# Low halves of twelve weight quarters computed on GpSimd inside the long-convolution layer, and one transposed block sent to other PSUM banks

## The reference, cut to what matters

```python
def hyena_mixer(h, w_in, short_w, short_b, f_w1, ..., f_skip, w_out):
    v, x1, x2 = jnp.split(depthwise_conv3(h @ w_in, short_w, short_b), 3, axis=-1)
    h_freq = hyena_filters(seq, f_w1, f_b1, f_w2, f_b2, f_w3, f_freq)   # divided by the sum of |filter|
    def long_conv(u, n):
        uf = u.astype(jnp.float32)
        y = jnp.fft.irfft(jnp.fft.rfft(uf, n=2 * seq, axis=1) * h_freq[:, n], n=2 * seq, axis=1)[:, :seq]
        return (y + uf * f_skip[n].astype(jnp.float32)).astype(u.dtype)
    z = x1 * long_conv(v, 0)
    z = x2 * long_conv(z, 1)
    return z @ w_out
```

## Time and profile before

| | us |
|---|---|
| median of 3 runs | 2025.57 |
| lowest, highest | 2024.82, 2026.21 |
| the profiled execution: time | 2027.8 |
| the profiled execution: span from first to last instruction | 2026.0 |
| PE busy in the span | 1970.8 |
| DVE busy | 1275.4 |
| ACT busy | 907.7 |
| GpSimd busy | 159.6 |
| load of a weight quarter (`w_raw`), median from issue to landing | 3.5 |

### The profile page before, as it was taken

One profiled execution on the slowest core, in us unless ns is written; L12 is line 12 of the kernel. 1 busy time (PEld: TensorE's weight loads), 2 busy tenths in 40 slices (PEclk: granted clock), 3 DMA queues, 4 the chain that ended last, 5 costly groups with the idle time before them and its releaser, 6 DMA issues.

```text
span 2026.0 us, 30699 instructions
## 1 busy us (share of the span) xinstructions
PE 1970.8 (97%) x12630; PEld 1608.2 (79%) x12630; DVE 1275.4 (63%) x1623; ACT 907.7 (45%) x1284; POOL 159.6 (8%) x198
## 2 busy tenths in 40 slices
PE   7999999999899999999999999999999999999999
PEld 6689788877678878888878678877767888898887
DVE  7874855567765565755767655577886555475554
ACT  4452344435444434444545444434434444444442
POOL 2242100000010010000002011002100000000000
PEclk9999999999999999999999999999998999999999
DMA  8411365646156654565565347553332566454554
GB/s 297 123 53 56 103 215 195 219 155 209 53 172 207 223 177 169 175 188 186 166 198 187 111 129 225 198 187 125 104 125 88 182 197 218 158 196 156 186 168 154
DMA packets 93044, 335.97 MB, mean 166 GB/s; under 512 B 11230, under 2 KB 11364, under 8 KB 92623
## 3 DMA queue, kind: packets, MB, share of 16 engines
q1 hardware_dynamic: 85824, 311.62, 46.3%
q0 software_dynamic: 7120, 22.95, 4.2%
HBM read 332.43 MB, written 1.05 MB: 165 GB/s over the span
## 4 chain that ended last, share of the span: by engine, by line
PE 87%; DVE 8%; ACT 2%; POOL 1%; issue 1%; DMA 0%; SPq 0%; DVEq 0%; ACTq 0%; POOLq 0%
PE acc L420 43%; PE acc L506 20%; PE acc L477 8%; DVE w_lo L1658 2%; PE acc L978 2%; PE aux L899 1%; PE aux L526 1%; PE aux L683 1%; POOL rstd L2494 1%; DVE w_spare_lo L1658 1%; PE aux L966 1%; PE aux L934 1%; POOL rstd L2497 1%; PE acc L670 1%; DVE operand_lo L1685 1%
## 5 line engine op out<-in xcount | busy, mean ns | idle before, releaser
L1658 DVE TENSOR_TENSOR w_lo<-w_raw,w_hi 128x1024 fp32r<-128x1024 f32 x552 | 670.3, 1225 | 531.4 <-ACT w_hi L1238 527.9
L1238 ACT ACTIVATE w_hi<-w_raw 128x1024 fp32r<-128x1024 f32 x552 | 580.2, 1059 | 719.2 <-PE acc L420 445.8
L420 PE MATMUL acc<-w_hi,operand_hi 128*128 128x512 f32 x1232 | 489.4, 397 | 14.6 <-DVE operand_lo L1832 12.4
L420 PE MATMUL acc<-w_hi,operand_lo 128*128 128x512 f32 x1232 | 482.3, 391 | 0.0
L420 PE MATMUL acc<-w_lo,operand_hi 128*128 128x512 f32 x1232 | 481.9, 391 | 0.0
L420 PEld LDWEIGHTS acc<-w_hi,operand_hi 128*128 128x128 f32 x1232 | 232.2, 188 | 63.3 <-DVE operand_lo L1832 12.2
L420 PEld LDWEIGHTS acc<-w_hi,operand_lo 128*128 128x128 f32 x1232 | 232.0, 188 | 49.0
L420 PEld LDWEIGHTS acc<-w_lo,operand_hi 128*128 128x128 f32 x1232 | 232.4, 189 | 46.6 <-issue 0.5
L506 PE MATMUL acc<-w_hi,hidden_hi 128*128 128x512 f32 x528 | 208.1, 394 | 0.0
L506 PE MATMUL acc<-w_hi,hidden_lo 128*128 128x512 f32 x528 | 206.1, 390 | 0.0
L506 PE MATMUL acc<-w_lo,hidden_hi 128*128 128x512 f32 x528 | 205.8, 390 | 0.0
(11 more groups left out here) (485 smaller groups left out, 2435.6 us busy)
## 6 DMA issues: line engine op xcount, KB each, us to landing
w_raw<-in_weights SPq DMA_DIRECT2D x552, 512.0 KB, 3.5
w_spare_raw<-in_weights SPq DMA_DIRECT2D x36, 512.0 KB, 5.2
ln_gain<-in_gains POOLq DMA_DIRECT2D x7, 512.0 KB, 4.9
bias_at<-in_rpb POOLq DMA_DIRECT2D x12, 256.0 KB, 5.1
ln_gain<-in_ln_g POOLq DMA_DIRECT2D x4, 512.0 KB, 4.3
ln_bias<-in_ln_b POOLq DMA_DIRECT2D x4, 512.0 KB, 5.6
vec_rw<-in_vec POOLq DMA_DIRECT2D x3, 512.0 KB, 6.7
l_rw<-in_lora SPq DMA_DIRECT2D x1, 1152.0 KB, 10.4
```

The source lines that it names most:

```text
L420: mm = pe.matmul(acc[:, 2 * pair + t, :], (ah, al)[x][:, kt, t * P:(t + 1) * P], weight(w, q + i)[:, kk * 512:(kk + 1) * 512], start=(kt = ...
L1238: act.activation(weight(0, q), raw_of(q), ACT.Copy).then_inc(hi_of(q)[0], 1)
L1658: dve.tensor_tensor(weight(1, q), raw_of(q), weight(0, q).bitcast(F32), ALU.subtract).then_inc(lo_of(q)[0], 1)
```

## The change

In the long-convolution layer the low parts of the quarters that DVE took at i = 1 and i = 3 of each block, twelve of 24, are computed by GpSimd. GpSimd's stream becomes: zero tap of filter 0, then for each block j the low part of (j, 1) and that of (j, 3), with the filter sums of filter 0 and the zero tap of filter 1 between those of block 0, and the sums of filter 1 between those of block 2. `turn_cv(2)` writes NEAR, the banks of block 2 itself, and waits only for the convolved block. The two waits on `dft_done` come together ahead of `idft(0, 0)`, and PE waits for the copy of the transposed block behind `idft(0, 0)`, since block 4 accumulates in NEAR.

```diff
+LOW_BY_POOL = (1, 3)
...
     def cv_banks(j):
-        return (HI, HI, HI, HI, LO, FAR)[j]
+        return (HI, HI, NEAR, HI, LO, FAR)[j]
...
                 elif (j, i) == (3, 2):
-                    free(m["dft_done"])
                     turn_cv(2)
                 elif (j, i) == (3, 3):
-                    free(m["dft_done"])
+                    free(m["dft_done"], m["dft_done"])
                     idft(0, 0)
+                    pe.wait_ge(m["cv_copied"], due(m["cv_copied"], 3))
                 elif (j, i) == (4, 0):
                     free(m["tap0_zeroed"])
-                    pe.wait_ge(m["cv_copied"], due(m["cv_copied"], 3))
                     spectrum(1, 1, 0)
...
             for j in range(6):
                 for i in range(4):
-                    ahead(q + 4 * j + i, 1)
+                    if i not in LOW_BY_POOL:
+                        ahead(q + 4 * j + i, 1)
                     inside_block(j, i)
                 convolve(j)
...
+            def low_part(j, i):
+                ahead_of = q + 4 * j + i + SLOTS
+                pool.wait_ge(*hi_of(ahead_of))
+                pool.tensor_tensor(weight(1, ahead_of), raw_of(ahead_of), weight(0, ahead_of).bitcast(F32), ALU.subtract).then_inc(lo_of(ahead_of)[0], 1)
+
+            zero_first_tap(0)
+            for j in range(6):
+                low_part(j, 1)
+                if j == 0:
+                    sum_sizes(0)
+                    zero_first_tap(1)
+                if j == 2:
+                    sum_sizes(1)
+                low_part(j, 3)
```

More of the change, by code:

```diff
@@ L2661, in near, with hyena, zero_first_tap @@
                 rsqrt(16)
-        def hyena():
-            for f in range(ORDER):
+        def hyena(q):
+            def zero_first_tap(f):
                 pool.wait_ge(m["filt_done"], due(m["filt_done"], 2))
@@ L2667, in hyena, with sum_sizes @@
                 due(m["filt_done"], 2)
+            def sum_sizes(f):
                 pool.wait_ge(m["filt_summed"], due(m["filt_summed"]))
@@ L2691, in _ @@
         ahead_of = {"moba": load_moba, "near": load_near}
-        inside = {"rwkv": rwkv, "near": near, "hyena": hyena}
+        inside = {"rwkv": lambda q: rwkv(), "near": lambda q: near(), "hyena": hyena}
         for n, kind in enumerate(layers):
             if kind in inside:
-                inside[kind]()
+                inside[kind](start[n])
             if n + 1 < len(layers):
```

## The result

The changed kernel takes 2028.76 us (median of 20 runs, 2026.33 to 2031.11), the one before 2025.45 us (median of 20). The ratio is 1.0013 with a 95% interval of 1.0008 to 1.0019: 2.6 us slower, between 1.6 and 3.9 (the two medians lie 3.3 us apart). Slow runs, such as two of the 20 before of 2799 and 2803 us, are left out of this ratio and of all that follow. The forecast was 2027.1.

The account below looks back on a forecast made before the run. PE bounds the kernel, so DVE counts only where PE waits on it. Terms: 0.48 (idft(0, 0) later) + 1.57 (slow clock) - 0.53 (wait at (5, 2)) = +1.5 us, on 2025.57 giving 2027.1 us; range 2020.9 to 2029.6.

Parts of the forecast that it names:

- That the wait moves: PE's 2.89 us wait before block 2's transposes goes; PE instead rests 4.95 us before idft(0, 0), released by products(0, 3).
- Exclusion between DVE with two SBUF operands and GpSimd: A DVE instruction with both operands in SBUF waits for a running GpSimd instruction to end, and the reverse.
- The rival without exclusion: GpSimd's work costs DVE nothing that matters; idft(0, 0) starts at 1458.25, -4.35 us, 2021.2 us; chance 0.12.
- fp32r on GpSimd: GpSimd's low parts, writing fp32r, take 2.38 us each, with 4.8 as upper bound, though no row showed that output.
- The rival of the slow low part: GpSimd's low part exceeds about 3.7 us; at 4.8 the layer's products come late, +7.5 us, 2033; chance 0.10.
- `idft(0, 0)` 0.48 us late: PE reaches idft(0, 0) at 1462.55, 0.48 us later than in the trace, after GpSimd's low parts hold up DVE.
- the third rival: GpSimd slips between the two sums of products(0, 1); idft(0, 0) starts at about 1463.4, +0.9 us on the forecast, 2028.0; chance 0.15.
- The hold of 1.9 us on DVE's low part (3, 0): GpSimd's low part (3, 1) holds the port 1450.47 to 1452.85, so DVE starts (3, 0) in effect at 1452.95.
- The slow clock: The same slow PE stretch comes again, now behind the wait at idft(0, 0): +1.57 us, bounds 0 and 2.1.
- the bound of 2.1: Upper bound on the slow clock's cost behind idft(0, 0): half of the 4.2 us stretch.
- (5, 2): PE's 0.59 us wait for products(1, 0) in quarter (5, 2) nearly goes: -0.53 us.
- The rival "DVE first": DVE reaches the last sum, L2383 of products(0, 3), ahead of GpSimd's low part (3, 3): -1.6 us, 2024.0; chance 0.20.

Follow-up runs that it names:

- e1: The changed kernel with the bank change alone, all 24 low parts on DVE and none on GpSimd; 2028.09 us, ratio 1.0008 to the kernel before.
- e3: The changed kernel with GpSimd's second-filter sums moved from ahead of low part (2, 3) to behind low part (3, 3); 2022.24 us, ratio 0.9982 to before.
- e7: e3 with the banks and waits of the kernel before the change; 2028.03 us, ratio 1.0007 to before.
- e10: e7 with low part (4, 1) back on DVE; 2021.14 us, ratio 0.9978 to the kernel before.
- e4: The changed kernel with each GpSimd low part computing 8 of its 1024 columns, the rest left out; 2025.13 us, ratio 0.9993 to before.
- e9: The changed kernel with five dummy matmuls on PE between the two waits ahead of idft(0, 0); 2026.35 us, ratio 1.0007 to before.
- e6: The changed kernel with low part (3, 3) back on DVE, behind products(0, 3); 2027.95 us, ratio 1.0007 to the kernel before.
- e2: The kernel before with the twelve low parts on GpSimd but the old banks and waits kept; 2027.39 us, ratio 1.0002 to before.

## Why the prediction was right

**That the wait moves, right and shown.** The transposes of block 2 start with no wait, `idft(0, 0)` rests 4.87 us (4.95 worked out), released by the last sum. e1 shows it without GpSimd, and e3 against e7 and e10 shows that at `idft(0, 0)` the bank change has 0.1 us to give even when DVE is on time.

**Exclusion between DVE with two SBUF operands and GpSimd, right and shown.** The Trainium skill's rule (SBUF — State Buffer, "Who interferes with whom") agrees with the blocked sums, 1.87 and 2.23 us for 0.69; one row that doesn't fit it, L2367, stands in the last section. The rival without exclusion is out: e4 takes the low parts' port time away, and `idft(0, 0)` comes 3.75 us earlier.

**fp32r on GpSimd, right.** Unblocked low parts take 2.35 to 2.41 us (2.38 taken). The rival of the slow low part is out.

**`idft(0, 0)` 0.48 us late, too small: it was 1.22.** The step that failed is "L2384 starts 0.47 us behind GpSimd's end ... GpSimd's low part (2, 3) takes 1447.55 to 1449.93". I gave two back-to-back DVE instructions the port in one piece. GpSimd's waiting low part got it between them, as the third rival had it (chance 0.15), and in `products(0, 0)` too, which no case had. By that rival `idft(0, 0)` comes about 1.4 us late, and its 2028.0 us are nearer to the measured time than the forecast. The path is the rival's too: PE waits 0.53 us before `dft(0, 3)`, so quarter (3, 3), its high part and GpSimd's low part (3, 3) all come later, that one by 0.66 us, and L2383 of `products(0, 3)` waits for its end. The hold of 1.9 us on DVE's low part (3, 0), which the text also gave, then did not come: (3, 1) ran while DVE convolved, and (3, 0) took 1.22 us at 1453.86. One mishap took the place of the other, and DVE ended (3, 0) within 0.3 us of the time worked out. That is luck, though little hung on it: L2383 of `products(0, 3)` stood 1.5 us in wait for low part (3, 3) after it.

**The slow clock, +1.57 charged, 2.04 found.** It was inside the bound of 2.1, and e9 shows it by removal. That a stretch of the same price comes again was a rough guess: rests of 1.93, 2.89, 3.35, 3.41, 3.98 and 4.87 us cost 1.76, 1.57, 2.83, 2.75, 2.83 and 2.04 us in e4, before, e6, e2, e1 and after, and the one of 3.10 us in e7 cost nothing. The length of the rest does not order them.

**(5, 2), right:** the wait is gone; 0.55 us for the 0.53 worked out.

The sum was +1.5 us, the trace has +2.71 up to the last piece: 0.74 more from the port between the sums and 0.47 more from the clock. The direction and the mechanism were right and both sizes too small. The rival "DVE first" (2024.0) is not what this kernel does, but e4, with the same rest of 1.9 us, bears out its clock term (1.76 us for 1.57).

What stays open: how much the order at the port varies between executions. The profiles show one execution each, and e7 shows that a fraction of a microsecond can turn it. By the last piece in the table e3, e7 and e10 should be 4.0, 1.1 and 3.3 us faster than before; their medians are 4.6 and 4.4 us faster for e3 and e10, but 2.0 us slower for e7. e7's profiled execution took 2025.72 us, 2.3 under its own median, so its layer may not be typical of its runs, and what the others look like wasn't seen. By the medians, then, the bank change makes e3 over 6 us slower, where the profiles have 2.8; e10 takes that back, which points at low part (4, 1), but that e7's other executions lose more there is not shown.

## What to carry to other kernels

Work handed to GpSimd is not free for the vector engine: where both read SBUF, look up at what time each piece becomes ready and which DVE instructions with two SBUF operands it can meet there, above all pairs on the way to a wait of PE. Moving two instructions that nobody wants soon (e3) was worth more than the whole change cost. When a wait is taken away, name the producer of the next one first: it sets the gain, and six of the seven rests of 1.9 to 4.9 us compared above cost 1.6 to 2.8 us of slow clock on top of their own length.

## What had not been expected of the hardware

**The port changes hands between instructions.** A waiting GpSimd instruction got it between two DVE instructions issued back to back, at L2384 (2.88 and 2.89 us for 0.68) and L2399 (3.47 us for 1.29). It works the other way as well: L2383 at 1445.74 ended at 1447.61, between GpSimd's L2676 and its low part, whose 2.85 us are 0.47 over its own 2.38. In these cases the two took turns. The next one is different.

**Small instructions wait as long as large ones.** L2367 with 8 columns takes 2.87 us at 1410.10 in the changed kernel, up to the end of GpSimd's low part (1410.57 + 2.36 = 1412.93). Before it took 0.18 us:

```profile
1409.91 0.18 DVE L2367 TENSOR_TENSOR token_scratch<-token_scratch,seam_hy 128x8 f32<-128x8 f32 x1
```

In both kernels GpSimd was in a memset when it was issued. In e4, where the low part queued behind the memset has 8 columns, it was issued 0.44 us into the memset, as in the changed kernel, and did not wait:

```profile
1408.71 0.18 DVE L2367 TENSOR_TENSOR token_scratch<-token_scratch,seam_hy 128x8 f32<-128x8 f32 x1
```

So the full-width low part behind the memset has to do with it, though by its row it starts 0.47 us after L2367. Why DVE, issued first, came second there, no run here shows.

**The length of a rest does not tell its price.** 1.93 us were followed by 1.76 us of slow clock (e4), but 3.10 us by none (e7, at a granted clock of 1.00), and 0.75 us by none (e3: 14.01 us for the work behind it).
